# First output projection, query projection and early expert blocks from split parts; selection and gate stage rearranged

## The chip, the core and the metric

One core of a Trainium2 chip runs the whole program. The time is the device time of one execution in microseconds; lower is better. All data are FP32. A matmul of plain FP32 operands is recorded as two matmul records. Where an operand is "split", it is held as a high part (the value rounded to the format FP32R) and a low part (the rest), and a product is the sum of three FP32R matmuls: high by high, high by low, low by high (TERMS in the code).

## The reference

Two blocks follow each other on 256 tokens (D = 1024). The first has two layers over the tokens x and 256 context tokens; its first ("even") layer joins a Fourier mixer and a window attention and multiplies the joined rows by ev_w_out. The second block ends in the PEER layer, product keys over 128 x 128 single-neuron experts:

```python
# even mixer, 512 columns (tokens and context)
o = concatenate([_fourier_mix(f), _window_attention(q, k, v, kc, vc, sink)], -1) @ w_out
x = x + g1 * o
# PEER, K = 16, 8 heads, 2 halves of 128 keys
q = (x @ wq).reshape(B, L, PEER_HEADS, 2, D_HALF)
s = einsum('blhpd,hpkd->blhpk', q, keys)
ts, ti = top_k(s, K)
cand = ts[..., 0, :, None] + ts[..., 1, None, :]
cs, ci = top_k(cand.reshape(B, L, PEER_HEADS, K * K), K)
e1 = take_along_axis(ti[..., 0, :], ci // K, -1)
e2 = take_along_axis(ti[..., 1, :], ci % K, -1)
g = softmax(cs)
act = gelu(einsum('td,tkd->tk', xt, u_tab[e1 * 128 + e2])) * g
out = einsum('tk,tkd->td', act, v_tab[e1 * 128 + e2])
```

The kernel doesn't gather experts. It builds, for each token, the 128 x 128 table of gates (gates[e, t] on the partition of the other key), and runs all 128 blocks of 128 experts for all 256 tokens.

## The kernel before

**Weights.** All weights come as one stream of blocks of 128 x 1024 (512 KB) through a ring of six slots in SBUF; SyncE issues the loads, each when its slot is released (STREAM, release). Unsplit blocks are read by TensorE from the ring itself (project, L531). For split ones ScalarE writes the high part (high, L1168), VectorE the low part (low, recorded at L1466), into one of three buffers; w_hi, w_lo and parts_begun are the semaphores between ScalarE, VectorE and TensorE, and a buffer is free for block n when block n - 2 has begun. ORD gives the running number of a split block over the whole program, and the buffer is ORD modulo 3.

**Attention of the even layer.** fourier() leaves its result in H (rows 0 to 3); attention(0) runs 16 units of a head pair and 128 queries, pipelined over TensorE, VectorE (mask, maximum, reciprocal, copy of the output at L1597), ScalarE (Exp, copies) and GpSimd (the scaling of the probabilities, L2090), with matmuls for later modulation vectors (ada) filled in between. ev_out then gives 8 tiles of 128 x 512 (L531); VectorE adds each to the residual, ScalarE squares it for norm(1).

**From w_out2 to the selection.** norm(5) on VectorE writes N2 (the normalized rows, 8 chunks of 128 x 256), one instruction a chunk. wq gives 16 tiles of 128 x 256 from N2, unsplit; after tiles 4, 8, 12 and at the end key_scores() multiplies four of them by the keys (L956) and ScalarE copies the scores. As soon as a quarter of the scores is there, VectorE selects: top() takes the 16 best of 128 for 8 rows (MAX8, FIND_INDEX8, MATCH_REPLACE8), the candidate sums CD are formed (four 128x256 instructions at L1466), the 16 best of 256 taken, the scores shifted by the maximum (two 128x32 instructions), the indices split by shifts and casts (L1459, L1947, L1948), and each rank matched with the key it stands for: compare (128x512, twice), multiply by the key numbers (128x256, four times), sum (L1963), twice per round. There are four rounds.

Under this TensorE runs the first AHEAD = 21 expert blocks ("peer0", unsplit, from N2); ScalarE applies gelu (L1364). It needs no gates yet. When both are done, ScalarE takes the exponentials, TensorE transposes the picks (L971), and the gate stage starts. Norm 4 and mix_first (L869) at the head of the mixer already do what the change brings to norm 5: each chunk is normalized by VectorE (L1463), its high part is made by ScalarE, its low part by VectorE, and TensorE runs two weight tiles interleaved, chunk by chunk.

**Gate stage.** 16 iterations of 16 tokens, in two halves of 8. For each token two one-hot rows: the second for 8 tokens in one VectorE instruction (second_rows, 128x1024), the first, times the gate, by VectorE (OWN1: four in the first half, three in the second; L1460), ScalarE (two each; L1388, L1393) and GpSimd (two and three; L2144, behind a staging copy, L2139). TensorE multiplies them (L991), four tokens to a bank. ScalarE copies the gates of expert blocks 21 to 127 (L1401, 428 elements), VectorE multiplies those of blocks 0 to 20 into the finished gelu values (84 elements a bank; the 21 blocks of a token lie 1 KB apart).

**Expert stage.** 21 spread blocks in a row (second table, L1028, 12 matmuls of 512 columns, weights and activations split), then for each of the other 107 experts an up block (L1016, 24 matmuls of 256 columns, split; n2p holds the parts of N2, whose low part GpSimd makes once, L2129) and a spread block.

## Time and profile before

| | us |
|---|---|
| median of 3 runs (2347.77 to 2350.08) | 2349.24 |
| the profiled execution | 2349.27 |
| its span, first to last instruction | 2347.5 |
| TensorE busy | 2202.4 (94%) |
| VectorE busy | 1377.6 (59%) |
| ScalarE busy | 892.8 (38%) |
| GpSimd busy | 160.6 (7%) |
| ev_out, on TensorE | 215 to 272 |
| norm 5, queries, early expert blocks | 1430 to 1573 |
| gate stage | 1578 to 1668 |
| expert stage | 1668 to 2336 |

Of the views of the profile four are used below. The chain that ended last lists, in order of time, start, length and name of the pieces of work that released each other. The table of stretches gives, for each stretch, the busy time of each engine, the granted TensorE clock (1.00 is 2.4 GHz) and what DMA did. The groups by line give the mean duration of one instruction of a form. The timelines give start, time, engine, line, operation, output and input, count, and in brackets the idle time before and what ended it; an "x8" is eight instructions in a row, with the time from the first start to the last end.

### The profile page before, as it was taken

Reading aid. Unit: us, or ns where it says so; the run is one execution under the profiler, and the core shown is the slowest. Engines: PE = TensorE matmul, PEld = TensorE weight load, DVE = VectorE, ACT = ScalarE, POOL = GpSimd, SP = SyncE. Lnnn points to the kernel's source line nnn. Section 1 sums busy time; section 2 is a strip of 40 time slices with the busy share of each in tenths; the row PEclk is TensorE's granted clock in tenths of the full one; section 3 lists DMA queues with packets and bytes.
Section 4 is the critical chain, followed back from the end, with each engine's and each line's share of the span. In section 5 each row is a group of like instructions: output and inputs, shape, how many; then the busy total and the mean of one; then the engine's idle time right before and its main releaser. Section 6 shows DMA issues by size and latency. Waiting matters only on the chain.

```text
span 2347.5 us, 36271 instructions
## 1 busy us (share of the span) xinstructions
PE 2202.4 (94%) x13050; PEld 1838.1 (78%) x13050; DVE 1377.6 (59%) x2465; ACT 892.8 (38%) x1389; POOL 160.6 (7%) x249
## 2 busy tenths in 40 slices
PE   5999899999989999999799899987899999999998
PEld 2754488878876658999797678877789999999997
DVE  2454344332269564654677532999766666666665
ACT  2334322222243363433476201228544444444443
POOL 0022000000013030000000000008300000000000
PEclk8999999999989999999899999999999999999999
DMA  7265232223262364555543233430255555555553
GB/s 289 76 239 206 73 106 91 97 81 108 94 149 85 105 228 144 181 174 174 179 153 117 78 107 126 135 134 0 90 188 187 188 184 190 182 190 184 188 187 117
DMA packets 92838, 340.62 MB, mean 145 GB/s; under 512 B 10409, under 2 KB 10436, under 8 KB 92496
## 3 DMA queue, kind: packets, MB, share of 16 engines
q1 hardware_dynamic: 89280, 325.10, 41.4%
q0 software_dynamic: 3472, 14.35, 2.0%
q8 instruction: 57, 0.93, 0.2%
q14 instruction: 29, 0.24, 0.0%
HBM read 338.36 MB, written 1.05 MB: 145 GB/s over the span
## 4 chain that ended last, share of the span: by engine, by line
PE 80%; DVE 13%; ACT 3%; issue 2%; DMA 1%; DVEq 0%; SPq 0%; POOL 0%; ACTq 0%; POOLq 0%
PE bank L755 19%; PE bank L1028 15%; PE bank L1016 13%; PE bank L531 11%; PE bank L782 8%; PE bank L883 3%; DVE main_zone L1463 3%; DVE main_zone L1538 2%; DVE first_w_parts L1466 1%; DVE tail_zone L1460 1%; PE bank L727 1%; PE bank L706 1%; PE bank L570 1%; PE bank L715 1%; DVE main_zone L1466 1%
## 5 line engine op out<-in xcount | busy, mean ns | idle before, releaser
L755 PE MATMUL bank<-act_parts,first_w_parts 128*128 128x512 f32 (+1 forms) x2928 | 561.2, 353 | 17.8 <-DVE act_parts L1463 17.2
L755 PEld LDWEIGHTS bank<-act_parts,first_w_parts 128*128 128x128 f32 x2928 | 475.3, 194 | 99.9 <-issue 17.5
L1466 DVE TENSOR_TENSOR first_w_parts<-weight_ring,first_w_parts 128x1024 fp32r<-128x1024 f32 x166 | 211.3, 1275 | 284.1 <-ACT first_w_parts L1168 283.6
L1028 PE MATMUL bank<-w_parts,a_parts 128*128 128x512 f32 x1536 | 370.5, 392 | 4.4 <-DVE a_parts L1466 3.4
L1466 DVE TENSOR_TENSOR w_parts<-weight_ring,w_parts 128x1024 fp32r<-128x1024 f32 x235 | 286.8, 1221 | 90.4 <-ACT w_parts L1168 90.4
L1028 PEld LDWEIGHTS bank<-w_parts,a_parts 128*128 128x128 f32 x1536 | 282.7, 189 | 59.5 <-issue 5.1
L1016 PEld LDWEIGHTS bank<-n_parts,w_parts 128*128 128x128 f32 x2568 | 322.1, 191 | 8.3
L1016 PE MATMUL bank<-n_parts,w_parts 128*128 128x256 f32 x2568 | 324.6, 283 | 0.0
L1168 ACT ACTIVATE w_parts<-weight_ring 128x1024 fp32r<-128x1024 f32 x235 | 248.0, 1056 | 199.5 <-PE bank L1016 159.1
L1168 ACT ACTIVATE first_w_parts<-weight_ring 128x1024 fp32r<-128x1024 f32 x166 | 175.0, 1057 | 248.4 <-PE bank L755 119.5
L531 PE MATMUL bank<-main_zone,weight_ring 128*128 128x256 f32 (+1 forms) x976 | 242.5, 410 | 1.5 <-DVE main_zone L1597 0.8
L531 PEld LDWEIGHTS bank<-main_zone,weight_ring 128*128 128x128 f32 x976 | 186.2, 192 | 54.6 <-issue 31.2
L782 PE MATMUL bank<-ffn_hidden_parts,first_w_parts 128*128 128x512 f32 (+1 forms) x1056 | 187.5, 341 | 6.3 <-DVE first_w_parts L1466 6.3
L782 PEld LDWEIGHTS bank<-ffn_hidden_parts,first_w_parts 128*128 128x128 f32 x1056 | 165.7, 194 | 28.1 <-issue 6.8
L883 PE MATMUL bank<-n_parts,mix_w_parts 128*128 128x272 f32 x1008 | 138.0, 299 | 12.1 <-DVE mix_w_parts L1466 12.1
L883 PEld LDWEIGHTS bank<-n_parts,mix_w_parts 128*128 128x128 f32 x1008 | 133.5, 196 | 18.8 <-DVE mix_w_parts L1466 15.7
L1466 DVE TENSOR_TENSOR bank<-bank,main_zone 128x256 f32<-128x256 f32 x107 | 70.6, 660 | 104.8 <-ACT bank L1420 104.8
L1420 ACT ACTIVATE bank<-bank 128x256 f32<-128x256 f32 x107 | 39.4, 368 | 184.5 <-PE bank L1016 184.5
L991 PE MATMUL bank<-second_rows,tail_zone 128*128 128x128 f32 x512 | 67.5, 287 | 22.3 <-DVE main_zone L1466 18.9
L991 PEld LDWEIGHTS bank<-second_rows,tail_zone 128*128 128x128 f32 x512 | 61.7, 198 | 28.3 <-DVE main_zone L1466 24.6
L570 PE MATMUL bank<-weight_ring,small_zone 128*32 128x512 f32 x384 | 59.1, 629 | 16.4 <-ACT small_zone L1208 8.8
L1182 ACT ACTIVATE tail_zone<-bank 128x512 f32<-128x512 f32 (+1 forms) x44 | 21.6, 491 | 128.1 <-PE bank L755 128.1
(217 smaller groups left out, 2014.9 us busy)
## 6 DMA issues: line engine op xcount, KB each, us to landing
weight_ring<-in_stream SPq DMA_DIRECT2D x618, 512.0 KB, 3.4
main_zone<-in_rel_bias POOLq DMA_DIRECT2D x6, 512.0 KB, 13.8
main_zone<-in_decay POOLq DMA_DIRECT2D x1, 1536.0 KB, 9.6
main_zone<-in_xT POOLq DMA_DIRECT2D x1, 1024.0 KB, 11.5
main_zone<-in_ctxT POOLq DMA_DIRECT2D x1, 1024.0 KB, 16.0
tail_zone<-in_rel_bias POOLq DMA_DIRECT2D x2, 512.0 KB, 26.0
tail_zone<-in_keysT POOLq DMA_DIRECT2D x1, 1024.0 KB, 5.1
out<-main_zone SPq DMA_DIRECT2D x2, 512.0 KB, 2.7
```

The lines of the kernel that those rows point to most:

```text
L531: mm = pe.matmul(o[:, 0:w], wb[:, k, :], rhs[:, k, :], start=(k == 0), stop=(k == DC - 1))
L570: mm = pe.matmul(bank[ADA_BANKS[phase][half]][strip:strip + 32, :], cond[:, k, 10 - 2 * row:42 - 2 * row], wb[:, half * 512:(half + 1) * 512],
L755: mm = pe.matmul(o[:, 0:w], wb[:, hw, k, :], fin[:, hx, k, 0:w], start=(k == 0 and n == 0), stop=(k == DC - 1 and n == 2))
L782: mm = pe.matmul(o[:, 0:w], wb[:, hw, b % 8, :], fhid[:, hx, k, 0:w], start=(k == 0 and n == 0), stop=(k == FC - 1 and n == 2))
L883: mm = pe.matmul(o[:, 0:LT], wb[:, hw, k, :], n0p[:, hx, k, :], start=(k == 0 and n == 0), stop=(k == DC - 1 and n == 2))
L991: mm = pe.matmul(bank[g][:, j * P:(j + 1) * P], one1[:, 4 * g + j, :], one2[:, 4 * g + j, :], start=True, stop=True)
L1016: mm = pe.matmul(bank[e % 3][:, 0:L], w[:, hw, k, :], n2p[:, hx, k, :], start=(k == 0 and n == 0), stop=(k == DC - 1 and n == 2))
L1028: mm = pe.matmul(acc[n][:, :], ap_[:, e % 3, ha, (n // 2) * P:(n // 2 + 1) * P], wp[(B + b) % PARTS][:, hw, (n % 2) * 512:(n % 2 + 1) * 51 ...
L1168: act.activation(parts[n % PARTS][:, 0, :], ring[:, (s % RING) * 1024:(s % RING + 1) * 1024], ACT.Copy).then_inc(w_hi, 1)
L1463: return dve.scalar_tensor_tensor(out=o, in0=a, scalar=s, in1=b, op0=op0, op1=op1)
L1466: return dve.tensor_tensor(o, a, b, op)
L1538: link(dve.reciprocal(r, r))
```

## The change

ev_out, wq and peer0 are added to SPLIT. For ev_out the Fourier rows go to a place of their own (FOUR); GpSimd makes their high and low parts during units 4 to 7 of the attention, VectorE makes those of the attention output as it copies it, ScalarE and VectorE make those of the weights. For wq and peer0 ScalarE makes the high parts and GpSimd the low parts. norm(5) writes n2p chunk by chunk, over ScalarE and VectorE, and the first two query tiles are interleaved. AHEAD goes from 21 to 37, so 37 expert blocks are made early and 91 in the expert stage, and the number of spread blocks in a row is 37. The rank matches work in two joined PSUM banks, with the rank numbers in a third; a compare covers both halves of the tokens at once. In the gate stage TensorE writes eight tokens to a pair of joined banks; one product of 8 x 37 elements on VectorE and one copy of 8 x 91 on ScalarE take the place of two each; VectorE makes three of the first rows in each half, ScalarE two, GpSimd three. The order in which the three weight buffers of the mixer are named is turned by one to fit the shifted ORD.

```diff
@@ constants
-AHEAD = 21
+AHEAD = 37
-OWN1 = (4, 3)
-OWNP = (6, 5)
+OWN1 = 3
+OWNP = 5
...
-SPLIT = ("ev_in", "ffn_gu0", "ffn_d0", "od_in", "ffn_gu1", "ffn_d1", "w_in2a", "w_in2b", "w_in2c", "w_in2d", "peer")
+SPLIT = ("ev_in", "ev_out", "ffn_gu0", "ffn_d0", "od_in", "ffn_gu1", "ffn_d1", "w_in2a", "w_in2b", "w_in2c", "w_in2d",
+         "wq", "peer0", "peer")
...
+        query_parts = {name: [[first, query_w_parts1, mix_w_parts1][(r - turn) % PARTS][:, :].rearrange("p (h n) -> p h n", h=2)
+                              for r in range(PARTS)] for name, first in (("wq", query_w_parts0), ("peer0", ahead_w_parts0))}
...
-        bank = [ctx.enter_context(nc.psum_tensor(f"bank{i}", [P, 512], F32)) for i in range(8)]
+        twins = [ctx.enter_context(nc.psum_tensor(f"banks{2 * i}", [P, 1024], F32)) for i in range(4)]
+        bank = [twins[i // 2][:, i % 2 * 512:(i % 2 + 1) * 512] for i in range(8)]
@@ TensorE
-            project_and_sum("ev_out", H, T, 1, 1)
+            pe.wait_ge(four_split, 4)
+            for m in range(DC):
+                wb = split_block(ORD["ev_out"] + m, None, owp)
+                o = bank_of(TILE["ev_out"] + m)
+                for c in range(DC):
+                    for n, (hw, hx) in enumerate(TERMS):
+                        mm = pe.matmul(o[:, 0:T], wb[:, hw, c, :], fin[:, hx, c, :],
+                                       start=(c == 0 and n == 0), stop=(c == DC - 1 and n == 2))
...
+                if m == 0:
+                    ada_turn(1)
+            norm(1)
+            spread_rstd(1)
...
+            def query_first():
+
+                wb = [split_block(ORD["wq"] + j, None, query_parts["wq"]) for j in range(2)]
+                o = [bank_of(TILE["wq"] + j) for j in range(2)]
+                for k in range(DC):
+                    pe.wait_ge(normed, DC * 5 + k + 1)
+                    for j in range(2):
+                        for n, (hw, hx) in enumerate(TERMS):
+                            mm = pe.matmul(o[j][:, 0:L], wb[j][:, hw, k, :], n2p[:, hx, k, :],
+                                           start=(k == 0 and n == 0), stop=(k == DC - 1 and n == 2))
...
+            def query_tile(name, j):
+
+                wb = split_block(ORD[name] + j, None, query_parts[name])
+                o = bank_of(TILE[name] + j)
+                for k in range(DC):
+                    for n, (hw, hx) in enumerate(TERMS):
+                        mm = pe.matmul(o[:, 0:L], wb[:, hw, k, :], n2p[:, hx, k, :],
+                                       start=(k == 0 and n == 0), stop=(k == DC - 1 and n == 2))
...
-            for j in range(16):
-                project("wq", 16, N2, L, j, j + 1, normed_by=5)
+            query_first()
+            for j in range(2, 16):
+                query_tile("wq", j)
                 if j % 4 == 0 and j >= 4:
                     key_scores(j // 4 - 1)
             key_scores(3)
 
-            project("peer0", AHEAD, N2, L)
+            for e in range(AHEAD):
+                query_tile("peer0", e)
...
-                for g in range(4):
-                    pe.wait_ge(oh1, at(sum(OWN1[:g // 2 + 1]), sum(OWN1)))
-                    pe.wait_ge(oh2, at(g // 2 + 1, 2))
-                    if g:
-                        pe.wait_ge(oh1_act, at(g // 2 + 1, 2))
-                    if g % 2:
-                        pe.wait_ge(oh1_pool, at(g // 2 + 1, 2))
+                for h in range(2):
+                    pe.wait_ge(oh1, at((h + 1) * OWN1, 2 * OWN1))
+                    pe.wait_ge(oh2, at(h + 1, 2))
                     if i is not None:
-                        pe.wait_ge(gate_copied, at(g - 3, 4))
-                    for j in range(4):
-                        mm = pe.matmul(bank[g][:, j * P:(j + 1) * P], one1[:, 4 * g + j, :], one2[:, 4 * g + j, :],
+                        pe.wait_ge(gate_copied, at(h - 1, 2))
+                    for j in range(8):
+                        if j == OWN1:
+                            pe.wait_ge(oh1_act, at(h + 1, 2))
+                        if j == OWNP:
+                            pe.wait_ge(oh1_pool, at(h + 1, 2))
+                        mm = pe.matmul(twins[h][:, j * P:(j + 1) * P], one1[:, 8 * h + j, :], one2[:, 8 * h + j, :],
                                        start=True, stop=True)
@@ ScalarE
...
+                    if l == 0 and i == PAIRS:
+                        for b in range(PARTS - 1):
+                            high("ev_out", b, None, owp)
...
+                    if l == 0 and c + PARTS - 1 < DC:
+                        high("ev_out", c + PARTS - 1, None, owp)
...
-                    act.activation(H[:, v // 2, (v % 2) * L:(v % 2 + 1) * L], bank[2 + v % 2][:, 0:L], ACT.Copy).then_inc(f2_copied, 1)
+                    act.activation(FOUR[:, v // 2, (v % 2) * L:(v % 2 + 1) * L], bank[2 + v % 2][:, 0:L], ACT.Copy).then_inc(f2_copied, 1)
...
             norm(5)
+            high("wq", PARTS - 1, None, query_parts["wq"])
...
                 last.then_inc(tile_free, 1)
+                name, b = ("wq", j + PARTS) if j + PARTS < 16 else ("peer0", j + PARTS - 16)
+                if j < 15:
+                    high(name, b, None, query_parts[name])
...
-            act.activation(n2p[:, 0], N2, ACT.Copy).then_inc(n2_high, 1)
+            high("peer0", PARTS - 1, None, query_parts["peer0"])
             gates = view(0, KEYS, L)
             for e in range(AHEAD):
                 b = tile("peer0", e)
                 act.activation(gates[:, e, :], b[:, 0:L], ACT.Gelu_apprx_tanh).then_inc(tile_free, 1)
+                if e + PARTS < AHEAD:
+                    high("peer0", e + PARTS, None, query_parts["peer0"])
...
+                act.activation(o, twins[h][:, :].rearrange("p (t e) -> p t e", t=8)[:, :, AHEAD:], ACT.Copy).then_inc(gate_kept, 1)
@@ VectorE
...
+                    if k >= 4:
+                        x = [n0p, n2p][k - 4]
+                        tt_(x[:, 1, c, :], d["out"][:, c, :], x[:, 0, c, :].bitcast(F32), ALU.subtract).then_inc(normed, 1)
...
+                        if l == 0:
+                            o = bank[4 + j % 2][:, 0:P]
+                            hi, lo = (fin[:, h, MIXC[0] + pair, qt * P:(qt + 1) * P] for h in range(2))
+                            dve.tensor_copy(hi, o).then_inc(o_hi, 1)
+                            dve.wait_ge(o_hi, j + 1)
+                            tt_(lo, o, hi.bitcast(F32), ALU.subtract).then_inc(o_copied, 1)
+                            if j >= PAIRS - PARTS + 1:
+                                low("ev_out", j - (PAIRS - PARTS + 1), None, owp)
+                            continue
...
+                    if l == 0 and m + PARTS - 1 < DC:
+                        low("ev_out", m + PARTS - 1, None, owp)
...
-            EQ = view(EQ0, QT, 2 * TOPK, TOPK)
+            EQ = twins[3][:, :].rearrange("p (t n k) -> p t n k", t=QT, n=2 * TOPK)
+            ranks = bank[3][:, 0:TOPK]
+            dve.tensor_copy(ranks, small("iota16")).then_inc(psum_ranks, 1)
+            dve.wait_ge(psum_ranks, 1)
...
+                    link(tt_(EQ, view(rank, QT, P)[:, :, span].unsqueeze(3).broadcast_to([P, QT, 2 * TOPK, TOPK]),
+                             ranks.unsqueeze(1).unsqueeze(1).broadcast_to([P, QT, 2 * TOPK, TOPK]), ALU.is_equal))
                     for tt in range(QT):
-                        last = tt_(EQ[:, tt], view(rank, QT, P)[:, tt, span].unsqueeze(2).broadcast_to([P, 2 * TOPK, TOPK]),
-                                   small("iota16").unsqueeze(1).broadcast_to([P, 2 * TOPK, TOPK]), ALU.is_equal)
-                    link(last)
-                    for tt in range(QT):
-                        for j in range(2):
-                            e = EQ[:, tt, j * TOPK:(j + 1) * TOPK, :]
-                            key = TIh[:, tt * PH + 2 * g + j, half, :]
-                            last = tt_(e, e, key.unsqueeze(1).broadcast_to([P, TOPK, TOPK]), ALU.mult)
+                        e = EQ[:, tt].rearrange("p (j n) k -> p j n k", j=2)
+                        key = TIh[:, tt * PH + 2 * g:tt * PH + 2 * g + 2, half, :]
+                        last = tt_(e, e, key.unsqueeze(2).broadcast_to([P, 2, TOPK, TOPK]), ALU.mult)
...
+                tt_(a, twins[h][:, :].rearrange("p (t e) -> p t e", t=8)[:, :, 0:AHEAD], a, ALU.mult).then_inc(gate_copied, 1)
@@ GpSimd
...
+                    if l == 0 and 4 <= i < 8:
+                        c = i - 4
+                        pool.wait_ge(f2_copied, 8)
+                        pool.tensor_copy(fin[:, 0, c, :], FOUR[:, c, :]).then_inc(four_hi, 1)
+                        pool.wait_ge(four_hi, c + 1)
+                        pool.tensor_tensor(fin[:, 1, c, :], FOUR[:, c, :], fin[:, 0, c, :].bitcast(F32),
+                                           ALU.subtract).then_inc(four_split, 1)
...
-            pool.wait_ge(n2_high, 1)
-            pool.tensor_tensor(n2p[:, 1], N2, n2p[:, 0].bitcast(F32), ALU.subtract).then_inc(n2_split, 1)
+            def low(name, b):
+
+                s, n = SLOT[name] + b, ORD[name] + b
+                pool.wait_ge(w_hi, n + 1)
+                w = query_parts[name][n % PARTS]
+                pool.tensor_tensor(w[:, 1, :], ring[:, (s % RING) * 1024:(s % RING + 1) * 1024], w[:, 0, :].bitcast(F32),
+                                   ALU.subtract).then_inc(w_lo, 1)
+
+            for b in range(16):
+                low("wq", b)
+            for b in range(AHEAD):
+                low("peer0", b)
```

## Rows read from the trace of the kernel before

**Rows 1.** Chain that ended last, pieces in order of time: start us, us, what.
```profile
95.11 5.50 PE bank L755 x24
...
223.90 48.18 PE bank L531 x112
...
1500.47 72.54 PE bank L531 x336
...
1745.84 2.75 PE bank L1028 x12
1748.59 2.87 PE bank L1016 x24
```

**Rows 2.** Stretches: length, busy us (count) of PE, PEld, DVE, ACT, POOL; clock, DMA, GB/s.
```profile
172.00:192.00 20.00, 19.16 (x164) 9.89 (x164) 14.39 (x54) 13.16 (x36) 7.31 (x12) 1.00 0.83 291
...
1457.00:1573.00 116.00, 115.51 (x558) 101.67 (x556) 113.66 (x504) 18.55 (x40) 4.52 (x1) 1.00 0.44 145
...
1578.50:1668.00 89.50, 67.64 (x515) 62.03 (x516) 86.22 (x208) 77.45 (x194) 71.90 (x146) 0.96 0.00 0
```

**Rows 3.** Groups by line and form: busy us, mean ns of one, idle before.
```profile
L1168 ACT ACTIVATE w_parts<-weight_ring 128x1024 fp32r<-128x1024 f32 x235 | 248.0, 1056 | 199.5 <-PE bank L1016 159.1 <-PE bank L1028 37.3 <-PE bank L1003 3.1
...
L1597 DVE COPY main_zone<-bank 128x128 f32<-128x128 f32 x32 | 9.0, 280 | 14.5 <-PE bank L727 14.3
```

**Rows 4.** Timelines at norm 4, all engines, and norm 5, VectorE and TensorE.
```profile
1127.40 0.91 DVE L1463 SCALAR_TENSOR_TENSOR main_zone<-tail_zone,small_zone,bank 128x272 f32<-128x272 f32 x2 [0.99 <-PE bank L610]
...
1128.98 7.67 PE L869 MATMUL bank<-n_parts,mix_w_parts 128*128 128x272 f32 x48 [1.62 <-DVE n_parts L1466]
...
1434.26 3.22 DVE L1463 SCALAR_TENSOR_TENSOR main_zone<-tail_zone,small_zone,bank 128x256 f32<-128x256 f32 x8 [1.95 <-PE bank L610]
...
1434.88 19.71 PE L531 MATMUL bank<-main_zone,weight_ring 128*128 128x256 f32 x80 [0.67 <-DVE main_zone L1463]
```

**Rows 5.** Timelines of VectorE and GpSimd in the selection.
```profile
1457.04 1.65 DVE L1892 MAX8 main_zone<-main_zone 128x8 f32<-128x128 f32 x8 [19.57 <-ACT main_zone L1351]
...
1476.47 0.29 DVE L1466 TENSOR_TENSOR main_zone<-main_zone 128x32 f32<-128x32 f32 x2
...
1477.62 1.29 DVE L1466 TENSOR_TENSOR main_zone<-main_zone,small_zone 128x512 f32<-128x512 f32 x2
1478.95 1.43 DVE L1466 TENSOR_TENSOR main_zone<-main_zone 128x256 f32<-128x256 f32 x4
...
1481.67 1.29 DVE L1466 TENSOR_TENSOR main_zone<-main_zone,small_zone 128x512 f32<-128x512 f32 x2
...
1502.98 4.52 POOL L2129 TENSOR_TENSOR n_parts<-main_zone,n_parts 128x2048 fp32r<-128x2048 f32 x1 [115.92 <-ACT n_parts L1360]
...
1505.14 2.52 DVE L1466 TENSOR_TENSOR main_zone<-main_zone 128x32 f32<-128x32 f32 x2
...
1572.71 1.22 DVE L1963 TENSOR_REDUCE main_zone<-main_zone 128x64 f32<-128x1024 f32 x1
```

**Rows 6.** Gate stage: timelines of GpSimd and VectorE, then two forms by line.
```profile
1587.81 0.31 POOL L2139 COPY small_zone<-tail_zone 128x2 f32 x2 [0.40 <-PE bank L991]
...
1590.67 0.31 POOL L2139 COPY small_zone<-tail_zone 128x3 f32 x2 [0.24 <-POOL tail_zone L2144]
...
1601.48 1.21 DVE L1466 TENSOR_TENSOR second_rows<-tail_zone,bank 128x1024 f32<-128x1024 f32 x1
...
1604.32 1.21 DVE L1466 TENSOR_TENSOR second_rows<-tail_zone,bank 128x1024 f32<-128x1024 f32 x1
...
1606.41 0.52 DVE L1466 TENSOR_TENSOR main_zone<-bank,main_zone 128x84 f32 x2
1606.84 1.21 DVE L1466 TENSOR_TENSOR second_rows<-tail_zone,bank 128x1024 f32<-128x1024 f32 x1
...
L1466 DVE TENSOR_TENSOR bank<-bank,main_zone 128x256 f32<-128x256 f32 x107 | 70.6, 660 | 104.8 <-ACT bank L1420 104.8
...
L1466 DVE TENSOR_TENSOR main_zone<-bank,main_zone 128x84 f32 x60 | 16.0, 316 | 0.0
```

119 lines of the change are left out of this document (68 added, 51 removed).

## The prediction

> **What bounds the kernel now.** Busy shares are averages and say nothing about a single stage, so I began with the chain of work that ended last. Its long pieces are TensorE's, and they give a price per block of each kind [rows 1]. Then the table of stretches, for the stages that the change touches, and last the timelines inside them. Four things are to be seen.
>
> First, the output projection ev_out (unsplit FP32) runs at 48.18/112 = 0.430 us per matmul record, 16 records a tile, so 6.88 us a tile. A split block of the same width, three terms by eight chunks, takes 5.50 us [rows 1].
> Second, 256 columns wide, a query or early expert tile takes 72.54/336 x 16 = 3.454 us unsplit; an expert block in the late loop, already split, takes 2.87 us [rows 1].
> Third, from 1457 to 1573 us TensorE (115.5 of 116) and VectorE (113.7) are both full [rows 2]: the 21 early expert tiles cover the selection of the sixteen best. The last tile ends at 1573.0, the last reduction of VectorE at 1572.71 + 1.22 = 1573.9 [rows 1, 5]. Two lanes end together, so what the change does to each has to be followed to the end.
> Fourth, in the gate stage, 1578.5 to 1668, VectorE is busy 86.2 of 89.5 us and TensorE 67.6 [rows 2]: VectorE sets the pace. After that TensorE alone does (late loop, 5.62 us for an up and a spread block, clock 1.00).
>
> **ev_out.** 8 tiles x (6.88 - 5.50) = -11.0 us, on the path. The parts of its weights (ScalarE high, VectorE low) lie beside TensorE: at 5.50 us a tile both engines have room, as they have now in the feed-forward blocks of the same width. What is paid ahead of it is in the attention. From 172 to 192 us TensorE is busy 19.16 of 20, VectorE 14.39, GpSimd 7.31 [rows 2]. VectorE gets one more subtraction of 128x128 a unit, near the 0.28 us of the present copy [rows 3] and a semaphore, some 0.38 us x 16. GpSimd gets four times a 128x512 copy and subtraction: 12 instructions cost 7.31 us there, 0.61 each, and a two-input one 4.52/4 = 1.13 [rows 2, 5], so 1.8 us in each of four units of 3 to 3.7 us. Both fit into idle time, but both sit in a loop of hand-overs between four engines. At the end of it ScalarE makes two weight parts (1.06 us each [rows 3]) before the last copies, and one subtraction stands before the first ev_out matmul. Lower bound 0, as no work is taken off the loop. Upper bound, if nothing is hidden, 16 x 0.38 + 2 = 8. I take +1.5, near the lower end, because TensorE bounds that stretch. Part: **-9.5** (-11 to -3).
>
> **Start of the query projection.** Now norm 5 hands out eight chunks after one instruction each: eight in 3.22 us, first matmul at 1434.88, five tiles (80 records) in 19.71 us [rows 4]. After, each chunk passes VectorE, ScalarE and VectorE again, and two tiles run interleaved, exactly as norm 4 and the first mixer tiles do: from 1127.40 to 1128.98 + 7.67 = 1136.65 us, 9.25 us, at 272 columns [rows 4]. At 256 columns I take 9.0: the two tiles end at 1434.26 + 9.0 = 1443.3. The third tile's parts are made only behind the norm (ScalarE 1.06, then GpSimd 2.26, below), so tiles three and four start some 0.3 and 0.7 us late. Tile five ends at 1443.3 + 3 x 2.87 + 1.0 = 1452.9, against 1454.4 now.
>
> **Wq and the early expert blocks on TensorE.** From the end of tile five to 1573.0 are 118.6 us: 32 tiles x 3.454 = 110.5, and 8.1 for the four turns of key scores and their waits. After: 48 tiles x 2.87 = 137.8, with the same 8.1, from 1452.9: end at 1598.8. That is **+25.8** (24 to 29), if the parts come in time. GpSimd now makes the low parts. Its one subtraction in this stage, 128x2048 of the same kind, took 4.52 us [rows 5], so 2.26 for a block, below TensorE's 2.87. From the end of block k the chain gelu or copy 0.4, high part 1.06, low part 2.26 takes 3.8 us with hand-overs and is wanted after two blocks, 5.74: hidden, with 1.9 us in hand. In exchange 16 blocks leave the late loop: 16 x 2.87 = **-45.9** (certain to 0.5; the spread blocks that go with them stay, 37 in a row in place of 21).
>
> **Selection on VectorE.** It starts 2.6 us behind tile five as now (1457.04), at 1455.5, and runs 116.9 us now [rows 5]. A ranks match per half costs 1481.67 - 1477.62 = 4.05 us: two compares 1.29, four products 1.43, a reduction 1.24. After, one compare of 1024 elements and two products of 512, in PSUM, then the reduction. The key rows of the gate stage, 128x1024 with one operand in PSUM, take 1.21 [rows 6], so PSUM costs nothing extra: 1.25 + 1.32 + 1.24 = 3.8, 8 x 0.22 = -1.8. Alone that would end at 1568.
>
> But the lanes now share something. At 1502.98 GpSimd began its subtraction. VectorE's MAX8 and FIND_INDEX8 in that time ran at their usual length. Then came a pair of 128x32 subtractions with both inputs in SBUF: 2.52 us, where the pair takes 0.29 in the round before; it ended as GpSimd did [rows 5]. So such an instruction waits for GpSimd's. That is 2.2 us of the present chain (clean: 114.6, and 112.8 after, ending at 1568.3). GpSimd will be busy 2.26 of every 2.87 us, 0.79 of the time. The rank matches are out of this, with one operand in PSUM. Left are, in each of four rounds, four candidate sums (1.43 us) and two shifts of the scores (0.29). A group that arrives at a random moment waits 0.79 x 1.13 = 0.9 us; the idle gap of GpSimd is 0.6 us, so the candidate sums are cut once or twice more, 2.26 each. A round: 0.9 + 3.4 + 0.9 = 5.2, four: 21 us. End at 1589, before 1598.8. Bounds: 4 x 1.8 = 7 us (nothing is cut), and 24 x 2.26 = 54 us (each of the 24 waits for a whole subtraction): 1575 to 1622. Cost in my sum: 0, covered by the 37 early blocks; the cover is 30 us thick.
>
> The Trainium skill ("SBUF — State Buffer", Who interferes with whom) tells the same of two SBUF inputs and adds copies, casts and tensor_scalar between SBUF tensors, as the loser of a lock. No row here has one of them under GpSimd's subtraction. By the rule ten more short instructions a round would be held (rival a); by the row alone, none.
>
> **Gate stage.** VectorE's half iteration with three key rows takes 1606.84 - 1604.32 = 2.52 us, of which the two gate products (84 elements each) are 0.43; the other half 2.84, sum 5.36 [rows 6]. The new product has 8 x 37 = 296 elements at the same stride. From 84 elements (316 ns) to 256 with a strided operand (660 ns) are 2.0 ns an element [rows 6]; two of 84 in 0.43 leave 0.05 fixed for each. So 296 cost 0.64, and VectorE's iteration is 2 x (2.52 - 0.43 + 0.64) = 5.5. GpSimd takes over a key row and has three in both halves. Such a half, from one staging to the next, lasts 1590.67 - 1587.81 = 2.86 us, and its 0.24 of idle is a wait on itself [rows 6]: 5.72 an iteration, the longest lane. 15 x (5.72 - 5.36) = **+5.4** (bounds: -2 if strided elements come cheaper and GpSimd's wait goes; +9 if each half adds both).
>
> **Sum.** -9.5 + 25.8 - 45.9 + 5.4, and -0.1 for roundings, = -24.3 us. The profiled execution took 2349.27 us (span 2347.5), the median is 2349.24, so no correction: **2325 us**. In other words: 8 tiles x 1.38, 37 tiles x 0.58, less the losses.
>
> **Rivals.**
> (a) VectorE's selection becomes the end of the stage. For it: 0.79 of GpSimd's time is taken, and the row shows a full wait. Against: 30 us of cover. If the ten short casts and scalar forms a round are held too, the candidate group costs 0.9 + 2 x 2.26 and the other 0.9 + 1.5 x 2.26, 9.7 a round, 39 in all: end at 1607, 9 us late, 2334 us. The case covers 2327 to 2345. This is how the rule of the Trainium skill's page above would come out here.
> (b) The lock turns against the change altogether: one VectorE instruction for each of GpSimd's subtractions. The place is 1455 to 1598 us, the price 2.26 us for each held instruction. With the 24 of the rows the end is at 1622, 24 us late, and the gain is gone: that is the point from which it decides, about 54 us of waits. If casts and scalar forms are held in the same way, 64 instructions in all, 142 us bring 142/(112.8 + 145) = 0.55 of the chain, the rest (51 us) runs alone: end near 1649, 2375 us, slower. Against it: candidate sums behind one another have no wait between them, and GpSimd has to wait for ScalarE's part each time.
> (c) GpSimd starves TensorE: its subtraction, held by VectorE in turn, takes over 2.87 us. 53 blocks; at 3.1 us +12, 2337 us. From 3.33 us the gain is gone. Against: VectorE's holding instructions sum to 7 us in 140.
> (d) Better than the sum: nothing shows in the attention, and the gate loop stays at 5.36: 2318 us.
>
> **Chances.** Forecast with its bounds (2317 to 2334): 0.64. (a) 0.17, (b) 0.08, of which 0.06 slower, (c) 0.06, (d) 0.05. The range 2316 to 2340 takes in the forecast, (d), most of (a) and half of (c). A difference under 0.2% (4.7 us) is about what a measurement of this kernel can't tell from none. Faster than 2344.5: 0.88; within: 0.05; slower: 0.07.
>
> **What would show it.** ev_out at 5.50 us a tile, and the attention no more than 2 us longer. Query and early expert tiles each 2.87 us apart, with no wait of TensorE on GpSimd. VectorE's last reduction before the last early tile, and 128x256 sums in SBUF now and then 2 us long, while compares in PSUM are not. Gate iterations of 5.7 us with GpSimd as the last. The first spread block some 22 us later than now (25.8 + 5.4 - 9.5), 37 of them, then 5.62 us for each of 91 experts. The forecast is wrong if TensorE stands for more than 5 us behind the last early tile, or if a tile takes over 3 us.

## The result and the profile after

The changed kernel takes 2322.10 us (median, 2321.16 to 2324.24), beside 2349.14 (2347.77 to 2350.08) for the kernel before on the same chip: a ratio of 0.9886, 95% interval 0.9872 to 0.9900. The forecast of 2325 us was 2.9 us too high. The profiled execution took 2322.46 us, its span is 2320.7, against 2347.5: -26.8 us.

The chain that ended last answers to [rows 1] (start us, us, what):

```profile
214.59 5.73 PE banks L836 x24
222.01 38.25 PE banks L836 x168
...
1481.31 106.56 PE banks L1018 x888
...
1796.88 2.89 PE banks L1081 x24
...
1808.92 2.75 PE banks L1093 x12
```

ev_out (now L836) runs at 38.25/168 x 24 = 5.46 us a tile, where [rows 1] had 6.88. The early expert tiles (L1018) take 106.56/37 = 2.88 us each, one behind the other, with no wait between them, where they took 3.45. Up and spread blocks cost what they did.

The stretches that answer to [rows 2]: the attention, the selection (80 us out of its middle), the gate stage. Columns as there.

```profile
172.00:192.00 20.00, 19.16 (x165) 9.45 (x164) 15.31 (x58) 12.35 (x34) 12.75 (x18) 1.00 0.88 301
...
1500.00:1580.00 80.00, 80.00 (x669) 80.00 (x668) 78.39 (x256) 36.67 (x56) 67.99 (x28) 1.00 0.55 184
...
1593.00:1688.00 95.00, 73.01 (x518) 63.46 (x519) 89.98 (x160) 71.70 (x162) 84.30 (x162) 0.97 0.00 0
```

TensorE's 19.16 us in the attention's stretch are the same to the hundredth, although GpSimd (12.75 for 7.31) and VectorE (15.31 for 14.39) do more there. In the selection TensorE has no idle time left, and GpSimd now works 67.99 of 80 us.

TensorE's own timeline, at the head and at the end of the early tiles (it answers to norm 5 in [rows 4]):

```profile
1424.63 7.51 PE L1005 MATMUL banks<-n_parts,query_w_parts 128*128 128x256 f32 x48 [1.57 <-DVE n_parts L1540]
1432.43 3.14 PE L1018 MATMUL banks<-n_parts,mix_w_parts 128*128 128x256 f32 x24 [0.29 <-POOL mix_w_parts L2222]
1435.75 4.46 PE L1018 MATMUL banks<-n_parts,query_w_parts 128*128 128x256 f32 x35 [0.17 <-POOL query_w_parts L2222]
...
1584.81 3.04 PE L1018 MATMUL banks<-n_parts,query_w_parts 128*128 128x256 f32 x24
1591.41 1.02 PE L1037 MATMUL banks<-small_zone,main_zone 128*128 128x128 f32 x6 [3.56 <-DVE main_zone L1540]
```

The two waits on GpSimd, 0.46 us together, are the only ones. Behind the last tile stands the same 3.56 us as before the change (1573.0 to 1576.55): ScalarE's gelu of the last tile, its table load and exponentials (L1444), three short VectorE instructions.

VectorE's selection answers to [rows 5], with GpSimd's rows of the same time:

```profile
1445.90 1.65 DVE L1975 MAX8 main_zone<-main_zone 128x8 f32<-128x128 f32 x8 [16.39 <-ACT main_zone L1423]
...
1477.34 1.65 DVE L1975 MAX8 main_zone<-main_zone 128x8 f32<-128x128 f32 x8
...
1499.64 0.29 DVE L1540 TENSOR_TENSOR main_zone<-main_zone 128x32 f32<-128x32 f32 x2
1499.85 2.65 DVE L1533 TENSOR_SCALAR main_zone<-main_zone 128x32 uint32<-128x32 uint32 x4
...
1503.01 1.23 DVE L1540 TENSOR_TENSOR banks<-main_zone,banks 128x1024 f32<-128x1024 f32 x1
1504.27 1.30 DVE L1540 TENSOR_TENSOR banks<-banks,main_zone 128x512 f32<-128x512 f32 x2
...
1510.72 1.65 DVE L1975 MAX8 main_zone<-main_zone 128x8 f32<-128x128 f32 x8
...
1520.60 2.13 DVE L2016 CAST main_zone<-main_zone 128x64 f32<-128x64 uint32 x2
1522.65 3.63 DVE L1540 TENSOR_TENSOR main_zone<-main_zone 128x256 f32<-128x256 f32 x4
...
1545.28 1.65 DVE L1975 MAX8 main_zone<-main_zone 128x8 f32<-128x128 f32 x8
...
1578.58 1.23 DVE L2046 TENSOR_REDUCE main_zone<-banks 128x64 f32<-128x1024 f32 x1
1590.10 0.42 DVE L2049 TENSOR_REDUCE main_zone<-main_zone 128x16 f32<-128x256 f32 x1 [10.29 <-ACT main_zone L1444]
```
```profile
1500.02 2.45 POOL L2222 TENSOR_TENSOR ahead_w_parts<-weight_ring,ahead_w_parts 128x1024 fp32r<-128x1024 f32 x1 [0.48 <-ACT ahead_w_parts L1234]
1502.89 2.40 POOL L2222 TENSOR_TENSOR query_w_parts<-weight_ring,query_w_parts 128x1024 fp32r<-128x1024 f32 x1 [0.43 <-ACT query_w_parts L1234]
...
1520.18 2.40 POOL L2222 TENSOR_TENSOR query_w_parts<-weight_ring,query_w_parts 128x1024 fp32r<-128x1024 f32 x1 [0.48 <-ACT query_w_parts L1234]
1523.06 2.60 POOL L2222 TENSOR_TENSOR mix_w_parts<-weight_ring,mix_w_parts 128x1024 fp32r<-128x1024 f32 x1 [0.48 <-ACT mix_w_parts L1234]
```

The selection runs from 1445.90 to 1579.8, 133.9 us, and then VectorE is idle for 10.29 us. The rank matches in PSUM (1503.01 to 1506.86, 3.85 us a half) keep their length while GpSimd works. The four small TENSOR_SCALARs at 1499.85 take 2.65 us and end as GpSimd's subtraction of 1500.02 does (1502.47); of the two casts at 1520.60 the first is held until that of 1520.18 ends (1522.58). In each of them GpSimd holds VectorE. VectorE holds GpSimd too, but little: beside the candidate sums of 1522.65 a subtraction takes 2.60 us. In most blocks GpSimd is idle for 0.48 us, waiting for ScalarE's high part, which in turn waits until TensorE has begun an earlier block: the gap is TensorE's 2.88 us less GpSimd's 2.40. It turns out to be what the result rests on.

The waits aren't spread at random. The four rounds begin at 1445.90, 1477.34, 1510.72 and 1545.28, so they last 31.44, 33.38, 34.56 and 34.5 us, where an unheld round takes 28.2 (in the run with the longest GpSimd work, below, the last round, behind GpSimd's end, takes 28.25). 34.56 us are twelve of TensorE's 2.88: VectorE has fallen into step with GpSimd's stream, and the same instructions are held again each round.

### The profile page after: what moved, and what is told of

Same layout as the page of the kernel before. It is cut to its first block, busy times and chain, and to the rows that moved or that the text cites. A ratio compares the mean times of both kernels' runs of the same rounds, so it can differ in the third digit from the quotient of the medians.

```text
span 2320.7 us, 36646 instructions
## 1 busy us (share of the span) xinstructions
PE 2173.6 (94%) x13410; PEld 1845.8 (80%) x13410; DVE 1385.8 (60%) x2394; ACT 930.6 (40%) x1409; POOL 304.2 (13%) x325
## 4 chain that ended last, share of the span: by engine, by line
PE 79%; DVE 12%; ACT 4%; POOL 2%; issue 2%; DMA 1%; SPq 0%; DVEq 0%; POOLq 0%; ACTq 0%
PE banks L778 19%; PE banks L1093 15%; PE banks L1081 11%; PE banks L805 8%; PE banks L1018 6%; PE banks L554 3%; PE banks L920 3%; DVE main_zone L1537 3%; DVE main_zone L1610 2%; PE banks L836 2%; POOL tail_zone L2243 2%; DVE first_w_parts L1540 1%; PE banks L729 1%; PE banks L750 1%; PE banks L593 1%
## 5 line engine op out<-in xcount | busy, mean ns | idle before, releaser
L778 PE MATMUL banks<-act_parts,first_w_parts 128*128 128x512 f32 (+1 forms) x2928 | 561.1, 353 | 18.0 <-DVE act_parts L1537 17.5
L778 PEld LDWEIGHTS banks<-act_parts,first_w_parts 128*128 128x128 f32 x2928 | 475.6, 194 | 99.8 <-issue 17.6
L1093 PE MATMUL banks<-w_parts,a_parts 128*128 128x512 f32 x1536 | 367.5, 392 | 4.3 <-DVE a_parts L1540 3.2
L1093 PEld LDWEIGHTS banks<-w_parts,a_parts 128*128 128x128 f32 x1536 | 283.9, 189 | 60.0 <-issue 5.0
L1081 PEld LDWEIGHTS banks<-n_parts,w_parts 128*128 128x128 f32 x2184 | 274.0, 192 | 7.0
L1081 PE MATMUL banks<-n_parts,w_parts 128*128 128x256 f32 x2184 | 276.1, 283 | 0.0
L805 PE MATMUL banks<-ffn_hidden_parts,first_w_parts 128*128 128x512 f32 (+1 forms) x1056 | 187.3, 341 | 6.3 <-DVE first_w_parts L1540 6.3
L805 PEld LDWEIGHTS banks<-ffn_hidden_parts,first_w_parts 128*128 128x128 f32 x1056 | 165.7, 194 | 27.9 <-issue 6.8
L920 PE MATMUL banks<-n_parts,mix_w_parts 128*128 128x272 f32 x1008 | 138.0, 299 | 12.1 <-DVE mix_w_parts L1540 12.1
L920 PEld LDWEIGHTS banks<-n_parts,mix_w_parts 128*128 128x128 f32 x1008 | 133.5, 196 | 18.8 <-DVE mix_w_parts L1540 15.7
L1057 PEld LDWEIGHTS banks<-second_rows,tail_zone 128*128 128x128 f32 x512 | 62.8, 196 | 32.5 <-issue 12.3
```

Of the source, the lines that this page charges most:

```text
L778: mm = pe.matmul(o[:, 0:w], wb[:, hw, k, :], fin[:, hx, k, 0:w], start=(k == 0 and n == 0), stop=(k == DC - 1 and n == 2))
L805: mm = pe.matmul(o[:, 0:w], wb[:, hw, b % 8, :], fhid[:, hx, k, 0:w], start=(k == 0 and n == 0), stop=(k == FC - 1 and n == 2))
L920: mm = pe.matmul(o[:, 0:LT], wb[:, hw, k, :], n0p[:, hx, k, :], start=(k == 0 and n == 0), stop=(k == DC - 1 and n == 2))
L1057: mm = pe.matmul(twins[h][:, j * P:(j + 1) * P], one1[:, 8 * h + j, :], one2[:, 8 * h + j, :], start=True, stop=True)
L1081: mm = pe.matmul(bank[e % 3][:, 0:L], w[:, hw, k, :], n2p[:, hx, k, :], start=(k == 0 and n == 0), stop=(k == DC - 1 and n == 2))
L1093: mm = pe.matmul(acc[n][:, :], ap_[:, e % 3, ha, (n // 2) * P:(n // 2 + 1) * P], wp[(B + b) % PARTS][:, hw, (n % 2) * 512:(n % 2 + 1) * 51 ...
```

## Experiments

Each edit is made on the changed kernel. Kernels under one heading shared a chip and its runs of the kernel before.

### How many blocks are early, and where the held instructions are

Before: 2349.71 us.

```diff
-AHEAD = 37
+AHEAD = 28
```

> The changed kernel with 28 early expert blocks in place of 37, all else as it is. Two-lane theory: TensorE's last early tile ends 9 x 2.87 = 25.8 us earlier (about 1562 on the clock of the changed kernel's trace), but VectorE's selection then ends last. It ended at 1579.8; with GpSimd done at about 1557 the two waits of the fourth round behind that go (4.4 us), so 1575.4, and the transposes start at 1576.6 in place of 1591.4: -14.8. Nine blocks more in the late loop: +25.8. Sum +11.0: 2333 us. Rival (a block costs TensorE 2.87 us early or late, and nothing else counts): 2322 us.

2332.57 us (2329.70 to 2335.77), ratio 0.9933 (0.9916 to 0.9950). TensorE's last tiles and what comes next:

```profile
1557.28 3.04 PE L1018 MATMUL banks<-n_parts,query_w_parts 128*128 128x256 f32 x24
1575.08 1.51 PE L1037 MATMUL banks<-small_zone,main_zone 128*128 128x128 f32 x6 [14.77 <-DVE main_zone L1540]
```

TensorE stands 14.77 us for VectorE, whose selection ends at 1573.7, and the nine blocks come back in the expert stage. So the early tiles are worth their number only as far as there is selection to cover.

To see which instructions are held, the shifted indices, their casts' inputs, were put into an unused part of a PSUM bank, with 28 early blocks kept so that VectorE is last and every microsecond of it counts:

```diff
-            CH, CL = view(CH0, NP, TOPK).bitcast(U32), view(CL0, NP, TOPK).bitcast(U32)
+            CH, CL = (bank[3][:, 64 + 256 * h:64 + 256 * h + 128].rearrange("p (t n) -> p t n", t=QT).bitcast(U32) for h in range(2))
...
```

> As e_ahead28, and the two shifted index tables of the selection (outputs of the shifts, inputs of the casts) lie in PSUM in place of SBUF; no instruction is added or taken away. Theory that single-input copies, casts and scalar forms between SBUF tensors are held by GpSimd's subtraction like those with two SBUF inputs: the held shifts and casts of rounds 1 to 3 go, 3 x 2.2 us, and the selection ends last here, so 2333 - 6.6 = 2326.5 us. Rival (only two SBUF inputs are held, the long casts in the trace are an accident of the record; or the wait moves to the next instruction): 2333 us, the time of e_ahead28.

2329.91 us (2329.41 to 2330.78), ratio 0.9917 (0.9901 to 0.9934). The intervals of the two ratios overlap, so the times alone don't tell these runs apart; the traces do: the selection takes 126.0 us in place of 129.4, and TensorE waits 11.33 us for it in place of 14.77. The groups of VectorE in the selection, first with 28 early blocks, then with the indices in PSUM as well (busy us, mean ns, idle before):

```profile
L1540 DVE TENSOR_TENSOR main_zone<-main_zone 128x256 f32<-128x256 f32 x17 | 10.5, 673 | 0.0
L1533 DVE TENSOR_SCALAR main_zone<-main_zone 128x32 uint32<-128x32 uint32 x16 | 6.2, 451 | 0.0
L2033 DVE CAST main_zone<-main_zone 128x32 f32<-128x32 uint32 x8 | 3.6, 449 | 0.1
```
```profile
L1540 DVE TENSOR_TENSOR main_zone<-main_zone 128x256 f32<-128x256 f32 x17 | 15.0, 934 | 0.0
L1533 DVE TENSOR_SCALAR banks<-main_zone 128x32 uint32<-128x32 uint32 x16 | 1.9, 181 | 0.0
L2033 DVE CAST main_zone<-banks 128x32 f32<-128x32 uint32 x8 | 1.5, 186 | 0.1
```

A scalar form or cast with one side in PSUM is not held (181 and 186 ns, the unheld length; the longest of the 32 took 0.19 us); with both in SBUF it is. That shows which instructions are held. The gain fell short of the expected 6.6 us, 3.4, because waits moved on: the scalar forms and casts lost some 8 us together, and the candidate sums behind them rose from 673 to 934 ns, by 4.4 us. An unheld group only arrives earlier at the next lock.

The matches themselves, back in SBUF:

```diff
-            EQ = twins[3][:, :].rearrange("p (t n k) -> p t n k", t=QT, n=2 * TOPK)
-            ranks = bank[3][:, 0:TOPK]
+            EQ = view(21504, QT, 2 * TOPK, TOPK)
+            ranks = view(21504 + 1024, TOPK)
```

> The changed kernel with the rank matches (the 128x1024 table and the 16 rank numbers) in SBUF in place of PSUM, same instructions. Theory of the held instructions: 24 more instructions with two SBUF inputs, 2.5 us in a row twice a round; each may wait for a subtraction of 2.4 us, and they hold GpSimd in turn. About 11 us more a round until GpSimd is through, at 1585 to 1590; selection ends near 1610, 20 us behind: 2342 us (2335 to 2355). Rival (PSUM gave only space; the cover is thick enough): 2322 to 2324 us.

2332.92 us (2331.72 to 2336.40), ratio 0.9933 (0.9915 to 0.9950). It is slower, as the theory has it, but the median lies below its range of 2335 to 2355, half way between its 2342 and the rival. A rank match of this kernel and GpSimd's rows beside it:

```profile
1508.35 8.99 DVE L1540 TENSOR_TENSOR main_zone<-main_zone 128x1024 f32<-128x1024 f32 x3
```
```profile
1511.12 2.87 POOL L2222 TENSOR_TENSOR query_w_parts<-weight_ring,query_w_parts 128x1024 fp32r<-128x1024 f32 x1 [0.48 <-ACT query_w_parts L1234]
1513.99 2.80 POOL L2222 TENSOR_TENSOR mix_w_parts<-weight_ring,mix_w_parts 128x1024 fp32r<-128x1024 f32 x1
```

Compare and two products take 8.99 us, where they take 2.5 in PSUM. The holding goes both ways: GpSimd's 2.40 become 2.87 and 2.80, and between the two it has no idle time left. The selection lasts 156.4 us, 22.5 more; 12.3 of them reach the transposes (TensorE waits 15.85 us for 3.56), the rest is cover. The second and third round grew by 12.2 and 11.5 us, as expected, the first by 5.1 only. The last took 28.2 us, since GpSimd was done (1582.64) before its first instruction that can be held: it lost even the 6.3 us of waits that it has in the changed kernel. This the expectation left out. So the PSUM banks of the change are worth some 11 us here.

Then the lock was made tighter by one more subtraction on GpSimd in every early block, each behind the one before:

```diff
...
+                pool.tensor_tensor(view(22528, 256), ring[:, (s % RING) * 1024:(s % RING) * 1024 + 256], w[:, 0, 0:256].bitcast(F32),
+                                   ALU.subtract).then_inc(pool_chain, 1)
                 pool.tensor_tensor(w[:, 1, :], ring[:, (s % RING) * 1024:(s % RING + 1) * 1024], w[:, 0, :].bitcast(F32),
```

> The changed kernel, but GpSimd makes one more subtraction of 128x256, into an unused place, before the low part of each of the 53 query and early blocks; nothing reads it. GpSimd's subtraction takes 2.40 us and it idles 0.47 of 2.88 us now. With some 0.65 to 0.7 more it needs 3.1 a block. Theory that GpSimd's own rate is the limit to TensorE: about 48 tiles x 0.2 = 10 us more, 2332 us, and TensorE waits on GpSimd each tile. Rival (three buffers give 1.9 us in hand, so an added 0.65 us is hidden): 2322 us.

2370.21 us (2366.56 to 2372.17), ratio 1.0085 (1.0067 to 1.0103): slower than the kernel before, and far from both expectations. TensorE lost some 6 us as a block took GpSimd 3.06. The rest is VectorE's: its selection takes 191.5 us, and most of that is in one row:

```profile
1538.51 55.12 DVE L2016 CAST main_zone<-main_zone 128x64 f32<-128x64 uint32 x1
```
```profile
1590.49 0.72 POOL L2225 TENSOR_TENSOR main_zone<-weight_ring,query_w_parts 128x256 f32<-128x256 f32 x1
1591.18 2.39 POOL L2227 TENSOR_TENSOR query_w_parts<-weight_ring,query_w_parts 128x1024 fp32r<-128x1024 f32 x1
```
```profile
1641.43 1.51 PE L1037 MATMUL banks<-small_zone,main_zone 128*128 128x128 f32 x6 [44.67 <-DVE main_zone L1540]
```

A cast that takes 0.19 us unheld took 55.12. It ended at 1593.63, as GpSimd's last subtraction did (1591.18 + 2.39 = 1593.57): it was held through 18 blocks in a row. TensorE then stood 44.67 us. So with GpSimd busy without a gap, a held instruction can starve. Others in the same trace got through between two GpSimd instructions, and why this one didn't the trace doesn't show.

### Where the cover ends, and what each remaining part is worth

Before: 2345.98 us (2340.99 to 2350.74, a wider spread than elsewhere); ratios are the better measure under this heading.

```diff
-AHEAD = 37
+AHEAD = 21
```

> This kernel computes only 21 expert blocks (84 query tiles) early, as the kernel before did, with split parts and the ranks matched in PSUM; everything else is the changed kernel. Theory (TensorE's cover decides): the early tiles end about 16 x 2.88 = 46 us sooner than with 37 blocks, at about 1541.7; VectorE's selection, whose waits end with GpSimd's parts, ends at about 1573.6, as with 28 blocks, so the transposes come at about 1574.8, 16.6 us sooner than in the changed kernel; the 16 blocks come back in the expert stage at 2.88 us each, 46.0 us. Sum +29.4 us on 2322: 2351 us, no faster than the kernel before although each tile is cheaper. Rival (the early count is of no account, a tile costs the same wherever it stands): 2322 us.

2351.97 us (2347.61 to 2354.98), ratio 1.0021 (1.0012 to 1.0031).

```profile
1571.45 1.52 PE L1037 MATMUL banks<-small_zone,main_zone 128*128 128x128 f32 x6 [33.08 <-DVE main_zone L1540]
```

With the old count of early blocks the whole change brings nothing, not even what it gains at ev_out: TensorE waits 33.08 us. The split of the tiles and the larger AHEAD are one change, not two.

```diff
-AHEAD = 37
+AHEAD = 34
```

> This kernel computes 34 expert blocks early in place of 37; everything else is the changed kernel. In the changed kernel TensorE ends its early tiles at 1587.7 and VectorE its selection at 1579.8: 7.9 us of cover to spare. Theory (the lead is TensorE's): 3 blocks fewer end TensorE 8.6 us sooner, at about 1579, level with the selection, and give the 8.6 us back in the expert stage: within 2 us of the changed kernel, 2322 to 2324. Rival (the selection is released by TensorE's or GpSimd's end, and follows it down): still 2322; rival (the spare cover is false and VectorE is already last): 2330 us.

2324.57 us (2321.66 to 2325.49), ratio 0.9897 (0.9880 to 0.9915), within the interval of the changed kernel. The last tile (1581.2) and the selection (1581.8) end within a microsecond of each other, and the 3.56 us to the transposes are the same. The spare cover of 37 blocks costs and gives nothing that this measurement can tell.

ev_out as in the kernel before, in attention, mixer rows and weights:

```diff
-SPLIT = ("ev_in", "ev_out", "ffn_gu0", "ffn_d0", "od_in", ...
+SPLIT = ("ev_in", "ffn_gu0", "ffn_d0", "od_in", ...
...
-            pe.wait_ge(four_split, 4)
-            for m in range(DC):
...
+            project_and_sum("ev_out", H, T, 1, 1)
```

> This kernel undoes the first output projection's part of the change alone: its weights and rows are not split into parts, and the attention's copies and the four-tap sums are written as in the kernel before. Theory: its eight tiles take 6.9 us each again in place of 5.5 (11 us), and VectorE loses the extra splitting beside the attention (0.3 to 1.5 us): +10 us, 2332 us. Rival (the splitting cost the attention all that the tiles gave): 2322 us. Rival (the stage behind starts on a transfer anyway): 2322 us.

2331.67 us (2326.93 to 2333.70), ratio 0.9929 (0.9909 to 0.9949), against 0.9886: 0.0043 x 2349 = 10 us. From the chain of this kernel:

```profile
214.29 7.13 PE banks L554 x16
223.11 48.18 PE banks L554 x112
```

ev_out ends at 271.29, 57.0 us after its start; split it takes 214.59 to 260.26, 45.7. From the first matmul of ev_in to that of ev_out are 154.8 us here and 155.6 in the changed kernel: the splitting costs the attention 0.8 us.

The gates' rows shared otherwise, ScalarE 3 and 2, GpSimd 2 and 3, in alternate groups:

```diff
-OWNP = 5
+OWNP = (6, 5)
...
```

> This kernel changes the share of the gates' one-hot rows alone: of every group's eight rows VectorE writes 3, ScalarE 3 in one group and 2 in the next, GpSimd 2 and 3, where the changed kernel has 3, 2 and 3 in each (GpSimd was the last in each period there). Theory (GpSimd's three rows set the period of 5.8 us for two groups): 2.9 + 2.0 us of GpSimd are no longer last, the period falls to about 5.5 us, over some 16 periods 4 to 5 us: 2318 us. Rival (ScalarE or the chain of copies holds the period at 5.8, or the added row of ScalarE makes it last): 2322 to 2325 us.

2320.81 us (2315.43 to 2321.95), ratio 0.9881 (0.9864 to 0.9898). It lies between the theory (2318) and the rival (2322 to 2325), and can't be told from the changed kernel across chips. So both were run together, below.

### The changed kernel beside the mixed shares, and GpSimd's gap made smaller

Before: 2349.00 us (2343.85 to 2350.43).

> The changed kernel itself, on one chip with the runs beside it, so that differences of a few microseconds can be read. Expected: 2322 us, or the same share below the kernel before as the first time, 0.989.

2321.83 us (2318.84 to 2325.74), ratio 0.9889 (0.9874 to 0.9905).

> The gates' one-hot rows shared as in the run with mixed shares, beside the changed kernel on one chip. That run's trace has a period of 5.50 us in place of 5.80 and the gate stage 3.6 us shorter (92.4 against 96.0). Theory (the stage lies in the chain, so its 3.6 us are the kernel's): 3.6 us below the changed kernel, 0.15%. Rival (the 3.6 us are given back to the first transfers or weights of the expert stage): level with it.

2318.09 us (2315.18 to 2319.88), ratio 0.9871 (0.9854 to 0.9888): 3.7 us below the changed kernel, with intervals that overlap. GpSimd in the gate stage, first of the changed kernel, then with mixed shares:

```profile
1646.16 0.31 POOL L2238 COPY small_zone<-tail_zone 128x3 f32 x2 [0.24 <-POOL tail_zone L2243]
...
1649.10 0.31 POOL L2238 COPY small_zone<-tail_zone 128x3 f32 x2 [0.31 <-POOL tail_zone L2243]
...
1651.97 0.31 POOL L2238 COPY small_zone<-tail_zone 128x3 f32 x2 [0.24 <-POOL tail_zone L2243]
```
```profile
1647.73 0.31 POOL L2238 COPY small_zone<-tail_zone 128x3 f32 x2 [0.24 <-POOL tail_zone L2243]
...
1650.29 0.39 POOL L2238 COPY small_zone<-tail_zone 128x2 f32 x2 [0.69 <-PE banks L1057]
...
1653.23 0.31 POOL L2238 COPY small_zone<-tail_zone 128x3 f32 x2 [0.24 <-POOL tail_zone L2243]
```

Two groups take 1651.97 - 1646.16 = 5.81 us in the one, with GpSimd waiting only for itself, and 5.50 in the other, where it waits for TensorE and VectorE has become the last. From the transposes to the first matmul behind the gates (L1069) are 96.0 and 92.5 us, and this 3.5 us is what the edit gives; the medians agree with it. The spans of the two executions profiled side by side differ by 7.8 us (2323.9 and 2316.1), but 4.3 of these arise ahead of w_out2, where the code is the same.

The subtraction added on GpSimd, cut to 64 and to 128 columns:

```diff
...
-                pool.tensor_tensor(view(22528, 256), ...
+                pool.tensor_tensor(view(22528, 64), ...
```

> This kernel has one more subtraction of 128x64 on GpSimd in every early block; by the line through the 128x256 form (0.73 us) and the 128x1024 form (2.40 us) it is put at 0.31 us. GpSimd's 2.40 us become about 2.67 in a period of TensorE's of 2.88: about 0.2 us of idle time are left in each. Theory (any idle time of GpSimd lets VectorE's held instructions through): the selection stays within 5 us of the changed kernel's 134, still under TensorE's cover, and the time at 2322 to 2324 us. Rival (what is lost is in proportion to what is added: 0.73 us gave 57.7 us): +24 us of selection, less 7.9 of cover: 2338 us.

2323.26 us (2321.04 to 2324.13), ratio 0.9893 (0.9877 to 0.9909).

> As with the 128x64 subtraction, with 128x128 in its place, put at 0.45 us: GpSimd works about 2.81 us in a period of 2.88, and under 0.1 us of idle time is left. Theory (one held instruction of VectorE passes in each gap or boundary of GpSimd's stream, and none starves while there is a gap): the selection grows by 5 to 25 us, so 2322 to 2340 us, and no instruction of VectorE is held over 6 us. Rival (a gap this small is as good as none): a held instruction starves until GpSimd ends, as in the kernel with 128x256: 2365 to 2370 us.

2334.56 us (2332.07 to 2337.55), ratio 0.9939 (0.9923 to 0.9955). The stretch 1500 to 1580 us, of the kernels with 64, 128 and 256 columns in this order (POOL is the fifth busy time):

```profile
1500.00:1580.00 80.00, 80.00 (x669) 80.00 (x669) 78.76 (x256) 37.16 (x56) 76.01 (x57) 1.00 0.55 184
```
```profile
1500.00:1580.00 80.00, 80.00 (x669) 80.00 (x669) 78.90 (x221) 36.66 (x57) 79.43 (x57) 1.00 0.56 183
```
```profile
1500.00:1580.00 80.00, 79.90 (x629) 76.57 (x628) 79.45 (x112) 37.37 (x53) 80.00 (x53) 1.00 0.52 172
```

| added on GpSimd | idle of 80 us | selection, us | TensorE waits for it, us | median, us |
|---|---|---|---|---|
| nothing | 12.0 | 133.9 | 3.6 | 2321.83 |
| 128x64 | 4.0 | 142.4 | 3.6 | 2323.26 |
| 128x128 | 0.6 | 155.4 | 14.8 | 2334.56 |
| 128x256 | 0.0 | 191.5 | 44.7 | 2370.21 |

(The last row is of the chip of the first experiments, the traced columns of the first row of the changed kernel's own trace.) The first 8 us of idle time cost the selection 8.5 us, which the cover takes, the next 3.4 cost 13, and the last half microsecond 36. For 64 columns the theory had said within 5 us of selection, and it was 8.5; its time of 2322 to 2324 us held. For 128 columns it had said 5 to 25 us of selection and 2322 to 2340 us, and both held. In neither run does an instruction starve: with 128 columns and 0.6 us of idle time left the longest held one took 2.67 us. The price is not in proportion to the work added; it runs away as the gap closes.

## Why the prediction came out as it did

**ev_out** (forecast -9.5). Tiles -11.0 forecast; 57.0 - 45.7 = 11.3 measured. Attention +1.5 forecast; +0.8 measured against the undone kernel, +0.3 against the kernel before. Taking the lower end was right: TensorE's busy time in the stretch didn't change at all.

**Start of the query projection and the early tiles** (forecast +25.8). Norm 5 began at 1423.09 and the two interleaved tiles ended at 1424.63 + 7.51 = 1432.14: 9.05 us for the 9.0 of the forecast. The two waits on GpSimd took 0.29 and 0.17 us, for 0.3 and 0.7. From there 2.88 us a tile. The transposes came at 1591.41 for 1576.55. That is +14.9, and since w_out2, the stage ahead of it, began 11.2 us sooner (1390.15 for 1401.35), the stretch up to them grew by 26.1. GpSimd's low part took 2.40 us, not the 2.26 of half a 128x2048 one, and never held TensorE but for the two waits; held by VectorE in turn it took up to 2.62: rival (c) didn't come.

**Expert stage** (forecast -45.9). From the first matmul behind the gates (1667.71 and 1687.40) to the end of the span are 679.8 and 633.3 us: -46.5.

**Selection** (forecast 21 us of waits, no cost). This is the step that was right in its sum and wrong in its parts. The selection took 133.9 us, 21.1 over the clean 112.8 (that value holds: the round behind GpSimd's end takes 28.25 us, four of them 113.0). But the forecast laid all 21 on the candidate sums and score shifts, 5.2 a round. By the means of the groups, held less unheld, these cost 17 x (0.805 - 0.42) + 8 x (0.298 - 0.18) = 7.5 us. The other 13.3 are TENSOR_SCALARs and casts (busy us, mean ns of one, idle before):

```profile
L1533 DVE TENSOR_SCALAR main_zone<-main_zone 128x32 uint32<-128x32 uint32 x16 | 8.4, 590 | 0.0
L2016 DVE CAST main_zone<-main_zone 128x64 f32<-128x64 uint32 x8 | 5.6, 738 | 0.1
L2033 DVE CAST main_zone<-main_zone 128x32 f32<-128x32 uint32 x8 | 3.6, 450 | 0.1
```

They took 173, 191 and 178 ns in the kernel before: 6.7, 4.4 and 2.2 us. The forms that no row of before had under GpSimd's work were the larger half. Nor do the groups arrive "at a random moment": from the third round on the same ones are held each time, and in the six traces with this selection, 34 or 37 early blocks and no work added on GpSimd, it lasts 133.8 to 133.9 us each time, though it begins anywhere from 1444.85 to 1457.01. The Trainium skill ("SBUF — State Buffer", Who interferes with whom) counts copies, casts and tensor_scalar between SBUF tensors among the forms that can take part in the lock; the trace and the run with the indices in PSUM agree with it. Rival (a), built on that rule, had them in and kept the oversized term beside them, hence its 39 us. Two errors of the same size and opposite sign met in the forecast: that its 21 us came out is luck. What saved the time in any case was the cover, and it was thinner than the text's 30 us, which is the distance to the unheld end (1568): 7.9 us between 1579.8 and 1587.7, where the forecast's own 1589 and 1598.8 leave 10.

**Rival (b)** stands nearer than its 0.08 said. Its mechanism is real: at 0.73 us more of GpSimd's work a block it takes all the gain and 20 us more (some 6 of them are TensorE's, at GpSimd's own rate). The argument against it, that GpSimd has to wait for ScalarE's part each time, was the right one, and its size was the 0.48 us of the rows above. The forecast took the gap as 0.6 without asking what happens at 0.

**Gates** (forecast +5.4). +4.8 measured (96.0 us for 91.2), with the period at 5.81 for 5.72 and GpSimd last, as said. The 296-element product took 0.76 us, not 0.64: the fixed part of 0.05 was read from two overlapping instructions, and the line through the means of 316 and 660 ns gives 0.74.

**Sum.** -24.3 forecast, -26.8 in the spans: -11.0 at ev_out (tiles -11.3, attention +0.3), +26.1, -46.5 and +4.8, all read off the traces, and two small terms that the forecast didn't have. ev_in's first matmul, which comes before every part of the change, stood at 58.96 us for 59.71, -0.75; and between ev_out and w_out2 some 0.6 us were lost. The largest single difference is the attention, 1.2 us cheaper than forecast. All this is finer than the executions repeat: in the other traces with the same code ahead of it the first query tile came 3.5 us earlier to 3.3 us later. That no other step hides a pair of errors isn't shown.

## What to carry to other kernels

Before a job is moved to GpSimd beside a working VectorE, list VectorE's instructions with all operands in SBUF, casts and scalar forms too, and the idle time that GpSimd keeps in each period; one operand in PSUM takes an instruction out of the list. Keep a gap in GpSimd's stream: with 4.0 us idle in 80, 0.14 a block, the time was that of the changed kernel within the noise, with none it was 48 us longer. Where two lanes end together, a cheaper step on one pays only if work is moved to fill it (21 early blocks: no gain; 34 and 37: 24 and 27 us, not told apart), and filling beyond that gained nothing here. Of a wait between two periodic streams ask whether they fall into step, before taking it as random.
